# Delta rule's output projection: norm gain moved into the weights, the gate product on GpSimd, the squares on VectorE, two weight units split in quarters

## The chip, the cores and the metric

The kernel runs on one core of a Trainium2 chip. The metric is the device time of one execution in microseconds (us), here the median of three runs. A core has TensorE (matrix products; PE in the profile, PEld for its weight loads), ScalarE (ACT), VectorE (DVE), GpSimd (POOL) and SyncE (SP), which here only issues DMAs. Each engine works through its own queue in order, and the queues meet only at semaphores.

## The reference, cut to what matters

The whole program is two transformer blocks over 16 + 512 = 528 tokens of width 1024. The change lies in the last part of the first layer, the output of the gated delta rule:

```
def gated_deltanet(h, w_in, w_conv, a_log, dt_bias, w_norm, w_out):
    ...
    o = chunk_gated_delta_rule(q, k, v, g, beta)          # (1, 528, 16 heads, 128)
    o = rms_norm(o, w_norm) * jax.nn.silu(z.reshape(b, t, GDN_V_HEADS, GDN_HEAD_DIM).astype(jnp.float32))
    return o.reshape(b, t, GDN_V_DIM).astype(h.dtype) @ w_out

def rms_norm(x, w):
    y = xf * lax.rsqrt(jnp.mean(xf * xf, axis=-1, keepdims=True) + RMS_EPS)
    return (y * w.astype(jnp.float32)).astype(x.dtype)
```

`w_norm` is one vector of 128 gains, the same for all 16 heads; `w_out` is 2048 x 1024. The result is added to the residual `h`. Everything is float32.

## The kernel before, in words

Features lie on the 128 partitions and the 528 tokens on the free axis, so one head's output is a tile of 128 x 528, `value(i)` for head i of 16, in `k.wide`. A float32 product is made of three products of rounded halves: weights and activations are each split into a high part (rounded by ScalarE) and a low part (the rest, by VectorE), and TensorE multiplies high by high, high by low and low by high (`product`, L174). Weights come in units of 128 x 2048 in a ring of four raw slots (`load_unit`, L130). `split_hi` (L151) and `split_lo` (L159) make the high and the low part of a unit, in two split slots.

`gdn_back` runs the delta rule itself. Near its end it replaces the spilled gate z in DRAM by z(1 + tanh(z/2)), which is twice silu(z), and it loads the first three units of `w_out` ahead.

`normed_down` (L2217) is the stage around the change. For each head i: a square of `value(i)` on ScalarE (`square`), its sum over the 128 features by two matmuls with a matrix of ones on TensorE (`total`, L2342), a logarithm and an exponential on ScalarE (`logarithm`, L2265, and `root`, L2269) which give 1/rms, value times gain times 1/rms on VectorE (`norm`, L2301), that times 0.5 times the loaded gate (`scale`, L2308) into `a`, then the high part of `a` on ScalarE (L2280) and the low part on VectorE (`low`, L2312). TensorE multiplies head i into output tile 0 (weight unit 0) as soon as its low part is there, and head i - 3 into output tile 1 (unit 1; `BEHIND` is 3), then issues `total(i+3)`:

```
            for kt in range(kts):
                pe.wait_ge(lo_ready, kt + 1)
                one(0, kt)
                if kt == BEHIND:
                    pe.wait_ge(k.lo_done, u0 + 2)
                if kt >= BEHIND:
                    one(1, kt - BEHIND)
                if kt + 3 < kts:
                    total(kt + 3)
```

Units 2 to 7 follow with all 16 heads each; their splits wait until the unit two before has been used. The order of each queue is written out by hand. The gates come by 16 DMAs into a ring of four slots, each behind the `scale` that frees its slot. The gain vector is loaded at the start of the stage.

Of the kernel before, what the change touches and what calls it, by code (L numbers as in the profile page):

```python
# [23 lines left out]
P = 128  # L24
# [27 lines left out]
def persistent(nc, ctx):  # L52

    k = Named(nc=nc)
    sb = lambda name, shape, dt=F32: ctx.enter_context(nc.sbuf_tensor(name, shape, dt))
    sem = lambda name: ctx.enter_context(nc.semaphore(name))
    k.stage_sems, k.last_sems, k.uncleared = ExitStack(), ExitStack(), []
    k.opened = []

    def stage_sem(name):  # L60

        k.opened.append(k.stage_sems.enter_context(nc.semaphore(name)))
        return k.opened[-1]
# [6 lines left out]
    k.eps = sb("eps", [P, 1])  # L70
    k.gains_in = sem("gains_in")
# [1647 lines left out]
def gdn_back(k, g, qkv, an, d, tmp, yt, chunk, out_unit):  # L1719
# [13 lines left out]
    with ExitStack() as ctx:  # L1733
# [15 lines left out]
                 "y5_done", "xz6_ready", "xz6_done", "y6_ready", "y6_done", "cut", "stepped", "one", "zeroed", "back", "tanh_done", "gated", "gate_stored")  # L1749
# [18 lines left out]
        def _(sp):  # L1768
# [415 lines left out]
def gdn(k, ins):  # L2184
# [3 lines left out]
    with ExitStack() as c:  # L2188
# [13 lines left out]
        gdn_back(k, g, qk, an, d, tmp, yt, chunk, gdn_out_unit(ins))  # L2202


def gdn_out(k, ins, then):
# [3 lines left out]
    normed_down(k, "gdn_out", gdn_out_unit(ins), ins["gdn_norm"].rearrange("o p -> p o"), k.z_d, o, k.h,  # L2209
# [7 lines left out]
def normed_down(k, name, cols, gain_src, gate_d, value, acc, later_gains, then=()):  # L2217
# [4 lines left out]
    with ExitStack() as ctx:  # L2222
        sb = lambda nm, shape, dt=F32: ctx.enter_context(nc.sbuf_tensor(f"{name}_{nm}", shape, dt))
        ahi, alo = sb("ahi", [P, kts, T], F32R), sb("alo", [P, kts, T], F32R)
        sq, rinv, z, a, gain = sb("sq", [P, 3, T]), sb("rinv", [P, 3, T]), sb("z", [P, ZS, T]), sb("a", [P, 2, T]), sb("gain", [P, 1])
# [3 lines left out]
        gain_in, squared, summed, log, inv, normed, scaled, hi_ready, lo_ready, added = (k.sem(f"{name}_{x}") for x in (  # L2229
            "gain_in", "squared", "summed", "log", "inv", "normed", "scaled", "a_hi", "a_lo", "added"))  # L2230
# [3 lines left out]
        ring = lambda u: (u0 + u) % RAW_SLOTS  # L2234

        @block.sync
        def _(sp):
            with nc.allow_non_contiguous_dma(reason="128 gains, feature on partitions"):
                sp.dma_start(gain[:, :], gain_src).then_inc(gain_in, 16)
# [14 lines left out]

        @block.scalar
        def _(act):
            def square(i):
                if i >= 3:
                    act.wait_ge(summed, i - 2)
                nc.scalar.activation(sq[:, i % 3, :], value(i), ACT.Square).then_inc(squared, 1)  # L2260
            def logarithm(i):
# [5 lines left out]
            def root(i):  # L2267
# [4 lines left out]
            square(1)  # L2272
            logarithm(0)
            root(0)
            square(2)
            logarithm(1)
# [12 lines left out]
            for u in range(n):  # L2289
                if u + 2 <= n:  # L2290
                    split_hi(k, act, u0 + u + 2, ring(u + 2), t0 + u + 1)
                if u >= 1:
                    tail.act(k, act, u - 1, added, u)
            tail.act(k, act, n - 1, added, n)
# [3 lines left out]
        def _(dve):  # L2298
            def norm(i):
                dve.wait_ge(inv, i + 1)  # L2300
                dve.scalar_tensor_tensor(out=rinv[:, i % 3, :], in0=value(i), scalar=gain[:, 0:1], in1=rinv[:, i % 3, :],  # L2301
                                         op0=ALU.mult, op1=ALU.mult).then_inc(normed, 1)
            def scale(i):
                dve.wait_ge(normed, i + 1)
                dve.wait_ge(z_in[i % ZS], 16 * (i // ZS) + 16)
                if i >= 2:
                    dve.wait_ge(lo_ready, i - 1)
                dve.scalar_tensor_tensor(out=a[:, i % 2, :], in0=rinv[:, i % 3, :], scalar=0.5, in1=z[:, i % ZS, :],  # L2308
                                         op0=ALU.mult, op1=ALU.mult).then_inc(scaled, 1)
# [3 lines left out]
            split_lo(k, dve, u0, ring(0))  # L2313
            dve.wait_ge(gain_in, 16)
            norm(0)
            for i in range(kts):
                if i >= 2:
                    low(i - 1)
                if i == BEHIND + 1:
                    split_lo(k, dve, u0 + 1, ring(1))  # L2320
                scale(i)
                if i == 0:
                    low(0)
                if i + 1 < kts:
                    norm(i + 1)
            low(kts - 1)
            for u in range(n):
                dve.wait_ge(k.tile_full, t0 + u + 1)
                dve.tensor_tensor(two(acc[:, u, :]), two(acc[:, u, :]), halves(k.ps[u % 4]), ALU.add).then_inc(added, 1)
                if u + 2 <= n:  # L2330
                    split_lo(k, dve, u0 + u + 2, ring(u + 2))
# [4 lines left out]
        def _(pe):  # L2336
# [16 lines left out]
            pe.wait_ge(k.lo_done, u0 + 1)  # L2353
# [1665 lines left out]
```

## Time and profile before

| | us |
|---|---|
| median of three runs | 1987.78 |
| the three runs | 1982.62, 1987.78, 1988.21 |
| span of the profiled execution, first to last instruction | 1984.7 |
| stage `normed_down`: first instruction to the end of its first two output tiles, in the span | 504.4 to 564.2 |

No device time of its own is listed for the profiled execution; its span stands 3.1 us under the median of the runs. Times in the trace count from the start of the span. A time in brackets behind a row is how long the engine sat idle before it, and the name behind the arrow is what it was waiting for. The column PEclk is the granted clock of TensorE as a share of 2.4 GHz. An instruction is often reported until some 0.08 us after its successor on the same engine has begun.

### The profile page before, as it was taken

How to read it: one execution, taken by the hardware profiler on the slowest of the kernel's cores; microseconds unless marked ns; L12 is line 12 of the kernel's file. 1: busy time of each engine (PE TensorE's matmuls, PEld its weight loads, DVE VectorE, ACT ScalarE, POOL GpSimd, SP SyncE). 2: the span in 40 equal slices, each digit the busy share in tenths (PEclk: the TensorE clock that was granted, in tenths of full speed). 3: DMA queues.
4: the chain of work that ended last, by engine and by line, in shares of the span. 5: the costliest groups of instructions: out<-in, count | busy, mean ns of one | idle time of the engine just before them, and what ended most of it. 6: DMA issues, size and time to landing. Idle time of an engine off the chain costs nothing. (4 is left out here: it accounts for less than half of the span.)

```text
span 1984.7 us, 31477 instructions
## 1 busy us (share of the span) xinstructions
PE 1891.1 (95%) x12756; PEld 1695.5 (85%) x12756; DVE 1076.6 (54%) x1786; ACT 871.5 (44%) x1437; POOL 111.1 (6%) x140
## 2 busy tenths in 40 slices
PE   7999999999799999999989998999999998899988
PEld 6999999898689999999989976778888885787766
DVE  6656689976543444444452277444444446853343
ACT  5557763677633433332243256343232333424442
POOL 0001150000000000000000020000000002000101
PEclk8999999999899999999999998999999998999989
DMA  7233462255342232222222232132323222411101
GB/s 175 86 92 105 130 190 71 63 160 167 100 118 84 86 98 94 85 85 97 93 62 90 71 83 84 64 106 85 106 85 104 86 85 66 125 46 43 49 17 43
DMA packets 211359, 182.58 MB, mean 92 GB/s; under 512 B 42736, under 2 KB 182000, under 8 KB 211240
## 3 DMA queue, kind: packets, MB, share of 16 engines
q1 hardware_dynamic: 211240, 180.93, 30.5%
q8 instruction: 83, 1.36, 0.3%
q14 instruction: 36, 0.29, 0.0%
HBM read 165.73 MB, written 15.16 MB: 91 GB/s over the span
## 5 line engine op out<-in xcount | busy, mean ns | idle before, releaser
L163 DVE TENSOR_TENSOR main_wlo<-raw,main_whi 128x2048 fp32r<-128x2048 f32 x106 | 244.1, 2302 | 348.0 <-ACT main_whi L156 348.0
L156 ACT CAST main_whi<-raw 128x2048 fp32r<-128x2048 f32 x106 | 201.7, 1903 | 408.4 <-PE ps L178 408.4
L178 PE MATMUL ps<-ffn_xhi,main_whi 128*128 128x264 f32 (+1 forms) x768 | 206.0, 322 | 6.6 <-DVE ffn_xlo L648 6.6
L178 PE MATMUL ps<-ffn_xhi,main_wlo 128*128 128x264 f32 (+1 forms) x768 | 206.1, 323 | 0.0
L178 PE MATMUL ps<-ffn_xlo,main_whi 128*128 128x264 f32 (+1 forms) x768 | 205.8, 322 | 0.0
L178 PE MATMUL ps<-ffn_ahi,main_wlo 128*128 128x264 f32 (+1 forms) x768 | 205.2, 322 | 0.0
L178 PE MATMUL ps<-ffn_alo,main_whi 128*128 128x264 f32 (+1 forms) x768 | 205.0, 321 | 0.0
L178 PE MATMUL ps<-ffn_ahi,main_whi 128*128 128x264 f32 (+1 forms) x768 | 203.9, 320 | 0.0
L178 PE MATMUL ps<-gdn_xhi,gdnf_whi 128*128 128x264 f32 x768 | 161.8, 292 | 4.4 <-DVE gdn_xlo L519 4.4
L178 PE MATMUL ps<-gdn_xlo,gdnf_whi 128*128 128x264 f32 x768 | 157.1, 286 | 0.0
L178 PE MATMUL ps<-gdn_xhi,gdnf_wlo 128*128 128x264 f32 x768 | 157.1, 286 | 0.0
L178 PEld LDWEIGHTS ps<-ffn_xhi,main_whi 128*128 128x128 f32 x768 | 129.0, 190 | 19.1 <-issue 7.5
L178 PEld LDWEIGHTS ps<-ffn_ahi,main_whi 128*128 128x128 f32 x768 | 127.9, 188 | 11.6
L178 PEld LDWEIGHTS ps<-ffn_xhi,main_wlo 128*128 128x128 f32 x768 | 128.4, 190 | 11.0
L178 PEld LDWEIGHTS ps<-ffn_xlo,main_whi 128*128 128x128 f32 x768 | 127.9, 189 | 11.5 <-issue 0.2
L178 PEld LDWEIGHTS ps<-ffn_ahi,main_wlo 128*128 128x128 f32 x768 | 127.7, 188 | 10.9
L178 PEld LDWEIGHTS ps<-ffn_alo,main_whi 128*128 128x128 f32 x768 | 126.9, 188 | 11.2
L361 DVE TENSOR_TENSOR h<-h,ps 128x528 f32<-128x528 f32 (+1 forms) x128 | 85.6, 692 | 80.2 <-PE ps L178 80.0
L178 PEld LDWEIGHTS ps<-gdn_xhi,gdnf_whi 128*128 128x128 f32 x768 | 121.6, 190 | 5.8 <-issue 4.8
L178 PEld LDWEIGHTS ps<-gdn_xlo,gdnf_whi 128*128 128x128 f32 x768 | 120.2, 190 | 0.0
L178 PEld LDWEIGHTS ps<-gdn_xhi,gdnf_wlo 128*128 128x128 f32 x768 | 119.8, 190 | 0.0
L1089 DVE SCALAR_TENSOR_TENSOR gdnf_y<-gdnf_pre,gdnf_convw,gdnf_y 128x528 f32<-128x528 f32 x96 | 82.6, 862 | 62.4 <-ACT gdnf_y L1062 60.0
(498 smaller groups left out, 3717.9 us busy)
## 6 DMA issues: line engine op xcount, KB each, us to landing
raw<-in_ff_up_dram SPq DMA_DIRECT2D x32, 1024.0 KB, 5.4
raw<-in_ff_down_dram SPq DMA_DIRECT2D x32, 1024.0 KB, 5.0
raw<-in_gdn_in_dram SPq DMA_DIRECT2D x24, 1024.0 KB, 5.5
raw<-in_w_in_dram SPq DMA_DIRECT2D x14, 1024.0 KB, 5.3
raw<-in_mlstm_in_dram SPq DMA_DIRECT2D x12, 1024.0 KB, 5.4
raw<-in_gdn_out_dram SPq DMA_DIRECT2D x8, 1024.0 KB, 7.2
gdn_v_spilled<-gdn_o SPq DMA_DIRECT2D x16, 264.0 KB, 2.2
gdn_z_spilled<-gdn_o SPq DMA_DIRECT2D x16, 264.0 KB, 3.5
```

The costliest lines, as they stand in the source:

```text
L156: k.nc.scalar.copy(k.whi[:, slot % SPLIT_SLOTS, :], k.raw[:, slot, :]).then_inc(k.hi_done, 1)
L163: eng.tensor_tensor(k.wlo[:, s, :], k.raw[:, slot, :], k.whi[:, s, :].bitcast(F32), ALU.subtract).then_inc(k.lo_done, 1)
L178: mm = pe.matmul(ps[:, b, 0:k.width], w, x[:, half], start=first and n == 0, stop=last and n == 2)
L361: dve.tensor_tensor(parted(k, acc[:, j, k.now]), parted(k, acc[:, j, k.now]), filled(k, k.ps[j % 4]), ALU.add).then_inc(s.down_free, 1)
L1089: dve.scalar_tensor_tensor(out=self.y[:, b, :], in0=self.pre[:, b, i:i + T], scalar=self.w[:, i, j:j + 1], in1=self.y[:, b, :], op0=ALU.mu ...
```

## The change

The gain vector no longer multiplies the activations. It lies along the rows of `w_out` within each head, so it is folded into the weights when they are split: the high part is the rounding of gain times weight (ScalarE, an activation with a scale vector), the low part is gain times weight minus that (VectorE). The factor 0.5 is put into the gain once by GpSimd, and the gain is loaded in `gdn_back`, behind its first loads on the SP queue. The product of value and gate moves to GpSimd, in place over the gate; VectorE makes the squares that ScalarE made, and one product of 1/rms with that result in place of two instructions. Units 0 and 1 are split in four quarters of 512 columns each (four heads' weights), one quarter at the start and one behind every second head, in the order unit 0, unit 1, unit 0, ...; TensorE waits for the quarter that it needs. `scale(i+1)` now stands ahead of `low(i)` on VectorE. Whole units 2 to 7 are split as before, with the gain.

```
 # gdn_back
+            with nc.allow_non_contiguous_dma(reason="128 gains, feature on partitions"):
+                sp.dma_start(k.out_gain[:, :], out_gain).then_inc(s.gain_in, 16)
...
+            pool.wait_ge(s.gain_in, 16)
+            pool.tensor_scalar(k.out_gain[:, :], k.out_gain[:, :], 0.5, None, ALU.mult).then_inc(s.gain_half, 1)
 # normed_down
+        quarter = lambda x: (x % 2, slice(UNIT // 4 * (x // 2), UNIT // 4 * (x // 2 + 1)))
...
+        @block.gpsimd
+        def _(pool):
+            for i in range(kts):
+                pool.wait_ge(z_in[i % ZS], 16 * (i // ZS) + 16)
+                pool.tensor_tensor(z[:, i % ZS, :], z[:, i % ZS, :], value(i), ALU.mult).then_inc(gated, 1)
 # ScalarE
-            square(0)
-            split_hi(k, act, u0, ring(0), t0)
...
+            weight_part(0)
             root(0)
             root(1)
             for i in range(kts):
                 act.wait_ge(scaled, i + 1)
                 nc.scalar.copy(hi(i), a[:, i % 2, :]).then_inc(hi_ready, 1)
                 if i + 2 < kts:
-                    logarithm(i + 2)
-                if i + 3 < kts:
-                    square(i + 3)
-                if i + 2 < kts:
                     root(i + 2)
-                if i == BEHIND - 1:
-                    split_hi(k, act, u0 + 1, ring(1), t0)
+                if i % 2 == 0 and i < 14:
+                    weight_part(i // 2 + 1)
 # VectorE
+            def square(i):
+                if i >= 3:
+                    dve.wait_ge(summed, i - 2)
+                dve.tensor_tensor(sq[:, i % 3, :], value(i), value(i), ALU.mult).then_inc(squared, 1)
...
+            def scale(i):
+                dve.wait_ge(gated, i + 1)
                 dve.wait_ge(inv, i + 1)
...
+                dve.tensor_tensor(a[:, i % 2, :], z[:, i % ZS, :], rinv[:, i % 3, :], ALU.mult).then_inc(scaled, 1)
...
+            square(0)
+            square(1)
+            weight_part(0)
+            square(2)
+            scale(0)
             for i in range(kts):
+                if i % 2 == 1 and i < 14:
+                    weight_part((i + 1) // 2)
                 if i + 1 < kts:
-                    norm(i + 1)
+                    scale(i + 1)
+                low(i)
+                if i + 3 < kts:
+                    square(i + 3)
+            weights(2)
 # TensorE
             for kt in range(kts):
+                if kt % 4 == 0:
+                    split(kt // 2)
                 pe.wait_ge(lo_ready, kt + 1)
                 one(0, kt)
-                if kt == BEHIND:
-                    pe.wait_ge(k.lo_done, u0 + 2)
                 if kt >= BEHIND:
+                    if (kt - BEHIND) % 4 == 0:
+                        split((kt - BEHIND) // 2 + 1)
                     one(1, kt - BEHIND)
```

## Rows read from the trace of the kernel before

**Rows 1.** Page, part 1: busy time of each engine, share of the span.
```profile
PE 1891.1 (95%) x12756; PEld 1695.5 (85%) x12756; DVE 1076.6 (54%) x1786; ACT 871.5 (44%) x1437; POOL 111.1 (6%) x140
```

**Rows 2.** Windows: busy PE, PEld, DVE, ACT, POOL; then PEclk, DMA share, GB/s.
```profile
506.00:516.00 10.00, 7.80 (x22) 5.63 (x22) 7.78 (x9) 7.47 (x13) 0.00 (x0) 0.51 0.89 266
516.00:523.00 7.00, 3.89 (x19) 2.72 (x18) 3.38 (x5) 6.80 (x11) 0.00 (x0) 0.97 0.29 77
523.00:530.00 7.00, 6.26 (x23) 5.54 (x24) 4.93 (x6) 2.81 (x6) 0.00 (x0) 0.52 0.27 80
530.00:561.00 31.00, 26.93 (x168) 22.17 (x168) 20.76 (x31) 21.92 (x39) 0.00 (x0) 1.00 0.45 121
```

**Rows 3.** Groups by line in the stage: busy us, mean ns; idle before, releaser.
```profile
L2301 DVE SCALAR_TENSOR_TENSOR gdn_out_rinv<-wide,gdn_out_gain,gdn_out_rinv 128x528 f32<-128x528 f32 x16 | 12.3, 767 | 13.3 <-ACT gdn_out_rinv L2269 13.3
L2308 DVE SCALAR_TENSOR_TENSOR gdn_out_a<-gdn_out_rinv,gdn_out_z 128x528 f32<-128x528 f32 x16 | 11.2, 702 | 0.1
L2265 ACT ACTIVATE gdn_out_rinv<-ps,eps 128x528 f32<-128x528 f32 x16 | 11.2, 700 | 10.4 <-PE ps L2342 10.4
L2260 ACT ACTIVATE gdn_out_sq<-wide 128x528 f32<-128x528 f32 x16 | 10.2, 636 | 0.9 <-PEq L97 0.9
L2269 ACT ACTIVATE gdn_out_rinv<-gdn_out_rinv 128x528 f32<-128x528 f32 x16 | 10.2, 635 | 0.1
```

**Rows 4.** Timeline of one head in the steady part of the stage.
```profile
545.45 1.05 PE L2342 MATMUL ps<-gdn_out_sq,ones 128*128 128x264 f32 x4
546.11 0.70 DVE L2312 TENSOR_TENSOR gdn_out_alo<-gdn_out_a,gdn_out_ahi 128x528 fp32r<-128x528 f32 x1
546.54 0.70 ACT L2265 ACTIVATE gdn_out_rinv<-ps,eps 128x528 f32<-128x528 f32 x1 [0.63 <-PE ps L2342]
...
546.87 0.51 PE L178 MATMUL ps<-gdn_out_ahi,main_whi 128*128 128x264 f32 x2 [0.36 <-DVE gdn_out_alo L2312]
...
548.45 1.05 PE L2342 MATMUL ps<-gdn_out_sq,ones 128*128 128x264 f32 x4
```

**Rows 5.** Timeline: `low` of heads 0, 5, 13 and 15.
```profile
511.48 0.71 DVE L2312 TENSOR_TENSOR gdn_out_alo<-gdn_out_a,gdn_out_ahi 128x528 fp32r<-128x528 f32 x1 [0.95 <-ACT gdn_out_ahi L2280]
...
531.33 0.70 DVE L2312 TENSOR_TENSOR gdn_out_alo<-gdn_out_a,gdn_out_ahi 128x528 fp32r<-128x528 f32 x1
...
554.94 0.70 DVE L2312 TENSOR_TENSOR gdn_out_alo<-gdn_out_a,gdn_out_ahi 128x528 fp32r<-128x528 f32 x1
...
559.54 0.71 DVE L2312 TENSOR_TENSOR gdn_out_alo<-gdn_out_a,gdn_out_ahi 128x528 fp32r<-128x528 f32 x1 [0.70 <-ACT gdn_out_ahi L2280]
```

**Rows 6.** Timeline: unit 2's low half, and the first product behind it.
```profile
563.34 2.29 DVE L163 TENSOR_TENSOR main_wlo<-raw,main_whi 128x2048 fp32r<-128x2048 f32 x1 [1.29 <-ACT main_whi L156]
...
565.69 0.51 PE L178 MATMUL ps<-gdn_out_ahi,main_whi 128*128 128x264 f32 x2 [1.46 <-DVE main_wlo L163]
```

**Rows 7.** SP's first DMA issues in the stage; the gate tile's times to landing.
```profile
504.49 0.33 SPq L2239 DMA_DIRECT2D gdn_out_gain<-in_gdn_norm_dram  x1
504.87 1.37 SPq L2246 DMA_DIRECT2D gdn_out_z<-gdn_z_spilled  x3
...
DMA to landing us min/median/max: 2.4/2.7/7.5
```

**Rows 8.** Timeline: GpSimd and VectorE, each with two inputs in SBUF.
```profile
278.63 1.29 POOL L1405 TENSOR_TENSOR gdnf_y<-gdnf_y,gdn_an 128x512 f32<-128x512 f32 x1 [1.26 <-DMA gdnf_y<-gdn_cum_rows]
280.25 2.97 POOL L1405 TENSOR_TENSOR gdnf_y<-gdnf_y,gdn_an 128x512 f32<-128x512 f32 x1 [0.33 <-DMA gdnf_y<-gdn_cum_rows]
...
278.72 3.35 DVE L163 TENSOR_TENSOR gdnf_wlo<-raw,gdnf_whi 128x2048 fp32r<-128x2048 f32 x1 [0.47 <-ACT gdnf_whi L156]
```

**Rows 9.** Groups by form elsewhere: instructions like the new ones.
```profile
L3854 POOL TENSOR_TENSOR fin_sqs<-fin_sqs,fin_sq 128x512 f32<-128x512 f32 x5 | 6.4, 1289 | 26.3 <-ACT fin_sq L3830 26.3
...
L633 ACT ACTIVATE ffn_xhi<-h,gains 128x528 fp32r<-128x528 f32 x8 | 5.1, 722 | 7.7 <-PEq L97 7.7
...
L648 DVE SCALAR_TENSOR_TENSOR ffn_xlo<-h,gains,ffn_xhi 128x512 fp32r<-128x512 f32 x8 | 5.4, 748 | 1.1 <-ACT ffn_xhi L633 1.1
```

More of the change, by code:

```diff
@@ L70, in persistent @@
     k.eps = sb("eps", [P, 1])
+    k.out_gain = sb("gdn_out_gain", [P, 1])
     k.gains_in = sem("gains_in")
@@ L2214, with normed_down @@
 ZS = 4
-def normed_down(k, name, cols, gain_src, gate_d, value, acc, later_gains, then=()):
+def normed_down(k, name, cols, gate_d, value, acc, later_gains, then=()):
     nc = k.nc
@@ L2234, in normed_down @@
         ring = lambda u: (u0 + u) % RAW_SLOTS
+        gain = k.out_gain[:, 0:1]
+        quarter = lambda x: (x % 2, slice(UNIT // 4 * (x // 2), UNIT // 4 * (x // 2 + 1)))
+        whole = lambda x: x - 6 + u0 + 1
         @block.sync
         def _(sp):
-            with nc.allow_non_contiguous_dma(reason="128 gains, feature on partitions"):
-                sp.dma_start(gain[:, :], gain_src).then_inc(gain_in, 16)
             for i in range(kts):
@@ L2253, in _, with weight_part, weights, root @@
             sp.wait_ge(k.gains_in, 16 * len(later_gains))
+        @block.gpsimd
[3 more added lines that the diff above has]
+                pool.tensor_tensor(z[:, i % ZS, :], z[:, i % ZS, :], value(i), ALU.mult).then_inc(gated, 1)
         @block.scalar
         def _(act):
[L2257 to L2261, printed above, removed]
+            def weight_part(x):
+                u, cs = quarter(x)
+                if x < 2:
+                    act.wait_ge(k.raw_landed[ring(u)], landed_value(u0 + u, ring(u)))
+                    act.wait_ge(k.tile_full, t0)
+                nc.scalar.activation(k.whi[:, ring(u) % SPLIT_SLOTS, cs], k.raw[:, ring(u), cs], ACT.Copy, scale=gain)\
+                    .then_inc(part_hi if x < 6 else k.hi_done, 1)
+            def weights(u, used):
+                act.wait_ge(k.raw_landed[ring(u)], landed_value(u0 + u, ring(u)))
+                act.wait_ge(k.tile_full, used)
+                nc.scalar.activation(k.whi[:, ring(u) % SPLIT_SLOTS, :], k.raw[:, ring(u), :], ACT.Copy, scale=gain)\
+                    .then_inc(k.hi_done, 1)
+            def root(i):
                 act.wait_ge(summed, i + 1)
@@ L2281, in _ @@
                 if i + 2 < kts:
-                    logarithm(i + 2)
-                if i + 3 < kts:
-                    square(i + 3)
-                if i + 2 < kts:
                     root(i + 2)
-                if i == BEHIND - 1:
-                    split_hi(k, act, u0 + 1, ring(1), t0)
[L2289 to L2294, printed above, removed]
+                if i % 2 == 0 and i < 14:
+                    weight_part(i // 2 + 1)
+            for u in range(2, n):
+                weights(u, t0 + u - 1)
+                if u >= 3:
+                    tail.act(k, act, u - 3, added, u - 2)
+            split_hi(k, act, u0 + n, ring(n), t0 + n - 1)
+            for u in range(n - 3, n):
+                tail.act(k, act, u, added, u + 1)
             tail.root(k, act)
@@ L2298, in _, with weight_part, weights @@
         def _(dve):
-            def norm(i):
-                dve.wait_ge(inv, i + 1)
[L2301 to L2305, printed above, removed]
+            def square(i):
+                if i >= 3:
+                    dve.wait_ge(summed, i - 2)
+                dve.tensor_tensor(sq[:, i % 3, :], value(i), value(i), ALU.mult).then_inc(squared, 1)
+            def weight_part(x):
+                u, cs = quarter(x)
+                if x < 6:
+                    dve.wait_ge(part_hi, x + 1)
+                else:
+                    dve.wait_ge(k.hi_done, whole(x))
+                w = ring(u) % SPLIT_SLOTS
+                dve.scalar_tensor_tensor(out=k.wlo[:, w, cs], in0=k.raw[:, ring(u), cs], scalar=gain,
+                                         in1=k.whi[:, w, cs].bitcast(F32), op0=ALU.mult, op1=ALU.subtract)\
+                    .then_inc(part_lo if x < 6 else k.lo_done, 1)
+            def weights(u):
+                s = ring(u) % SPLIT_SLOTS
+                dve.wait_ge(k.hi_done, u0 + u + 1)
+                dve.scalar_tensor_tensor(out=k.wlo[:, s, :], in0=k.raw[:, ring(u), :], scalar=gain,
+                                         in1=k.whi[:, s, :].bitcast(F32), op0=ALU.mult, op1=ALU.subtract).then_inc(k.lo_done, 1)
+            def scale(i):
+                dve.wait_ge(gated, i + 1)
+                dve.wait_ge(inv, i + 1)
                 if i >= 2:
                     dve.wait_ge(lo_ready, i - 1)
-                dve.scalar_tensor_tensor(out=a[:, i % 2, :], in0=rinv[:, i % 3, :], scalar=0.5, in1=z[:, i % ZS, :],
-                                         op0=ALU.mult, op1=ALU.mult).then_inc(scaled, 1)
+                dve.tensor_tensor(a[:, i % 2, :], z[:, i % ZS, :], rinv[:, i % 3, :], ALU.mult).then_inc(scaled, 1)
             def low(i):
@@ L2352, in _, with split @@
                 total(i)
-            pe.wait_ge(k.lo_done, u0 + 1)
+            def split(x):
+                if x < 6:
+                    pe.wait_ge(part_lo, x + 1)
+                else:
+                    pe.wait_ge(k.lo_done, whole(x))
             for kt in range(kts):
+                if kt % 4 == 0:
+                    split(kt // 2)
                 pe.wait_ge(lo_ready, kt + 1)
                 one(0, kt)
-                if kt == BEHIND:
-                    pe.wait_ge(k.lo_done, u0 + 2)
                 if kt >= BEHIND:
+                    if (kt - BEHIND) % 4 == 0:
+                        split((kt - BEHIND) // 2 + 1)
                     one(1, kt - BEHIND)
```

37 lines of the change are left out of this document (12 added, 25 removed).

## The prediction

> **What bounds the kernel now.** I read the page first: TensorE is busy 95% of the span [rows 1], so time can be saved only where it waits. The windows around the edited stage show such a place. From 530 to 561 us TensorE is busy 26.93 of 31 us at full clock; from 506 to 516 and from 523 to 530 it runs at about half its clock (0.51 and 0.52), the second time after a stretch (516 to 523) in which it had only 3.89 us of work in 7 [rows 2]. The groups of the stage then give each instruction's price [rows 3], and the timeline of one head gives the loop. There neither engine is full: ScalarE waits 0.63 us for TensorE's total, TensorE waits 0.36 us for `low` [rows 4]. The bound is a chain through all queues: total, logarithm, exponential, the VectorE steps, product, total. `low` of head 5 starts at 531.33 and that of head 15 at 559.54 [rows 5]: 28.2 / 10 = 2.82 us a head, 5.64 for two. TensorE's own work for a head is 1.05 (total) and two products; from 546.87 to the next total at 548.45 these take 1.58 after a wait [rows 4]; I take 1.46 without one, as the first matmuls behind a wait report 0.51 and the others 0.41. So 2.51 is its floor, and at most 0.3 us a head is to be had once the clock is up.
>
> The sum is made against the span of 1984.7; the median of the runs is 3.1 us above it, and I carry the difference over to the median. A measurement of this kernel can tell about 0.3% from no change, that is 5.96 us.
>
> **The change part by part.**
>
> *Work by engine.* ScalarE loses 16 squares of 0.636 and the whole splits of units 0 and 1, and gains eight quarters. A scaled rounding of 528 columns takes 0.722 [rows 9]; I take 0.71 for 512. VectorE loses `norm` (0.767) and gains a square, taken at `scale`'s 0.70 [rows 3]: even. Its quarters cost 0.75, the row of the same instruction at 512 columns [rows 9], against 2.29 for a whole unit [rows 6]: 8 x 0.75 = 6.0 against 4.6, so 1.4 us more over the stage. GpSimd gets 16 products. It takes 1.29 for 512 columns [rows 9], so about 1.3.
>
> *The new loop, without GpSimd.* What matters is the order. `low(i)` stands behind `scale(i+1)`, which needs the root of head i+1; at every odd i a quarter stands in front of both, and that quarter's high part stands on ScalarE behind that same root. Queued behind them are the next square on VectorE and the next `hi` on ScalarE, and TensorE waits for `low(i)`. From the end of `total(i+1)`: handoff 0.04, logarithm 0.70, handoff 0.04, exponential 0.635, quarter's high part 0.71 less 0.09 overlap, handoff 0.04, quarter's low part 0.75 less 0.08, `scale` 0.70 less 0.08, `low` 0.70: sum 4.07. (The handoff is the gap between a releaser's end and the start behind it: the total ends at 546.50, the logarithm starts at 546.54 [rows 4].) From the end of `low` to the end of the total that closes the loop: 0.05 + 1.58 + 1.05 = 2.68. Together 6.75 us, and it closes every two heads, since that total is `total(i+3)`. Before it was 5.64. So each pair of heads loses 1.1 us although no engine has more work than time: VectorE has 6 x 0.62 + 0.67 = 4.4 of 6.75.
>
> *Stretch by stretch, without GpSimd.* (a) To head 0's `low`: the gain's DMA no longer stands ahead of the gates (0.38 us [rows 7]), so gate 0 is issued at 504.49 and lands at about 507.2 with the median 2.7; its product with the value takes 1.3, then `scale(0)`, and `low(0)` must wait for `scale(1)`, whose gate lands a little later. That gives `low(0)` at 511 to 512.5 against 511.48: 0. (b) Heads 0 to 5 took 19.85 us before [rows 5], with a whole split between them and the second cold spell. The new loop makes it two loops of 6.75 and one head of 3.4, 16.9; but the first cold spell stays, and at half clock TensorE's 2.51 becomes about 5 for each head that has both products. I take -1.5, with 0 and -3 as ends. (c) Heads 5 to 13: four pairs, 4 x 1.1 = +4.4. (d) Behind head 13 there are no quarters, squares or gates left. Before, `low` of 13 ended at 555.64 and the two tiles at 564.2, 8.56 us; the nine products left are 9 x 0.735 = 6.6, with waits about 7. I take -1.5. (e) Units 2 to 7: the split of unit 2 is exposed now (TensorE waits 1.46 [rows 6]) and gets the scaled forms, 0.09 on ScalarE (0.722 with a scale vector [rows 9] against 0.635 for an activation of such a tile without one [rows 3]) and at most 0.06 on VectorE: +0.15. The others lie behind 16 x 0.735 = 11.8 us of products each. Sum: 0 - 1.5 + 4.4 - 1.5 + 0.15 = +1.6.
>
> *GpSimd and VectorE together.* At 278.72 VectorE began a 2048-column subtraction 0.09 us after GpSimd had begun a product of 1.29. It took 3.35; the same form takes 2.29 [rows 6, 8]. GpSimd's next product began at 280.25, ended at 283.22 and so ran 2.97, of which 1.15 lay after VectorE's end at 282.07 [rows 8]. So here one waits until the other is through, and each meeting costs 1.06 to 1.15 us. Every VectorE instruction of the new loop has two inputs in SBUF. VectorE's 4.4 and two GpSimd products (2.2) fill 6.6 of 6.75, so the products cannot all miss the chain. Ends: nothing (all in gaps) and 16 x 1.1 = 17.6 (all on the chain). The chain uses VectorE for 2.0 of each 6.75, and the products start when a gate lands, at no fixed phase; I take 2.0 / 6.75 of 17.6, some 5, less what the last heads absorb and what the cold start covers: +3.5.
> The Trainium skill (SBUF — State Buffer, Reading the diagram) says that the port pair which GpSimd and VectorE share is an exclusive lock, which a VectorE instruction with two SBUF inputs takes against a GpSimd instruction that reads SBUF. By this rule all 16 products exclude VectorE, as in my sum; without it the sum would be +1.6. The trace agrees, with 3.35 for 2.29.
>
> *Costed at nothing.* The gain's load and its halving in `gdn_back`: one DMA on SP behind loads that are followed by a wait for spilled gates, and one tiny GpSimd instruction on an idle engine; if that cover were gone it would cost one landing, 2.4 to 7.5 [rows 7]. Gates: a slot is free four heads (13 us) ahead, and landing plus product take 2.7 + 1.3. Loads of units 4 to 7 follow the same gates on SP and have more than 30 us.
>
> Forecast: 1.6 + 3.5 = +5.1, so 1984.7 + 5.1 = 1989.8 of span, 1992.9 as a median.
>
> **The rivals.**
>
> *A, the forecast:* the two-head loop with the quarters in it, and the meetings. With its ends (stretch b -3 to 0, meetings 1.5 to 7) +1.6 to +9: 1989 to 1997.
>
> *B, the meetings cost nothing,* since the products fall into VectorE's gaps of 2.35 us a loop. +1.6: 1989.4. For: the gaps are there. Against: 6.6 of 6.75.
>
> *C, TensorE becomes the bound (faster).* The small quarters keep it fed, its clock rises at 516 and never falls, and the queues run ahead. From 512.2: three heads of 1.8 and thirteen of 2.51, three products: 512.2 + 5.4 + 32.6 + 2.2 = 552.4, plus 2 for the cold start, against 564.2: -10, 1978. For: the old stretch at 0.35 a head over the floor and the cold spell at 523. It decides if `low` of odd heads comes within 2.5 us of the total before last; by rows 3, 4 and 9 it takes 4.07. If the quarters alone slip off the chain, loops are 5.4 to 5.7, and the result is near -3.
>
> *D, the clock falls again.* TensorE's share in the new loop is 5.0 / 6.75 = 0.74 against 0.87 before, with one gap of about 1.7 us in each pair. The spell at 523 followed 3.89 / 7 = 0.56 [rows 2]. A spell of 7 us at half clock takes in 7 / 5.0 = 1.4 heads, each 5.0 - 3.4 = 1.6 us longer than the loop: 2.2 a spell, and two or three more spells add 4 to 7. +9 to +12: 1997 to 2000. Against: at 0.87 in this stage, and through a head with 0.36 us of idle time in it, the clock held [rows 2, 4].
>
> *E, no effect:* 1987.8, if the gains at both ends cancel the loop. It lies between B and C.
>
> **How the numbers follow.** A 0.52, B 0.11, C 0.12, D 0.14, E 0.11. The time is A's, 1992.9. 80% range: it leaves out C's far half and D's upper end: 1983 to 1999. A's own range is 1989 to 1997. Bounds of no change are 1981.8 and 1993.7. Faster: C less its weak form, 0.10. Slower: D, and somewhat under half of A, 0.38. Same: the rest, 0.52.
>
> **What the profile after would show.** `low` of even and odd heads in pairs, unevenly spaced, with about 7 us per pair between 530 and 555; VectorE idle until ScalarE's quarter; a quarter-sized VectorE instruction or a `scale` of 1.5 us or more where a GpSimd product overlaps; GpSimd products of 1.3, some 2; TensorE at about 0.72 in the stage; unit 2's products starting at about 570 instead of 565.7; everything behind that shifted alone. I would be wrong if `low` came every 2.5 us (C), if the total ran at half clock behind 530 (D), or if another stage moved.

## The result and the profile after

| | us |
|---|---|
| changed kernel, median of 14 runs | 1993.49 (1991.04 to 1997.76) |
| kernel before, median of 14 runs on the same chip | 1985.81 (1981.9 to 1993.4) |
| ratio | 1.0041, 95% interval 1.003 to 1.0051 |
| span of the changed kernel's profiled execution | 1994.0 |

The changed kernel is slower by 0.41%, 7.7 us between the medians. The forecast was 1992.9. It had a chance of 0.52 on "within 0.3%", and the result lies just beyond that bound. In every profiled run of the experiments the device time stands 1.7 us above the span, so the profiled execution of before took about 1986.4. A profile is one execution and can lie several us from the median: 2.2 above it for after, 7.1 below it for the second profile of before, 5.8 below it for "VectorE's quarter behind `low`".

The busy times of the page, beside [rows 1]: TensorE's is the same, VectorE's is 9.6 us more, ScalarE's 5.7 less and GpSimd's 23.5 more:

```profile
PE 1891.5 (95%) x12756; PEld 1697.6 (85%) x12756; DVE 1086.2 (54%) x1792; ACT 865.8 (43%) x1427; POOL 134.6 (7%) x157
```

The windows that answer to [rows 2] (same columns). The stage begins 3.8 us later in this profile: ScalarE's first instruction of it starts at 508.19, where it started at 504.36.

```profile
506.00:516.00 10.00, 3.77 (x18) 2.53 (x16) 7.41 (x11) 5.70 (x10) 4.29 (x3) 0.94 0.69 203
516.00:523.00 7.00, 5.12 (x17) 3.90 (x17) 7.00 (x7) 3.05 (x6) 5.52 (x4) 0.50 0.41 130
523.00:530.00 7.00, 4.00 (x14) 2.56 (x14) 5.72 (x6) 4.04 (x7) 2.75 (x2) 0.85 0.14 40
530.00:561.00 31.00, 23.51 (x131) 20.69 (x132) 19.29 (x30) 17.54 (x29) 11.60 (x8) 0.89 0.27 74
```

Between 530 and 561 us TensorE was busy 26.93 of 31 at full clock before. Now it is busy 23.51, at a granted clock of 0.89. From 516 to 523 VectorE is busy the whole 7.00 us with only seven instructions.

The groups of the stage that answer to [rows 3] (busy us, mean ns, then idle time before and its releaser):

```profile
L2266 POOL TENSOR_TENSOR gdn_out_z<-gdn_out_z,wide 128x528 f32<-128x528 f32 x16 | 24.2, 1523 | 180.5 <-DMA gdn_out_z<-gdn_z_spilled 180.5
...
L179 PE MATMUL ps<-gdn_out_ahi,main_whi 128*128 128x264 f32 x76 | 18.9, 332 | 19.6 <-DVE gdn_out_alo L2338 18.0 <-DVE main_wlo L2328 1.6
...
L2335 DVE TENSOR_TENSOR gdn_out_a<-gdn_out_z,gdn_out_rinv 128x528 f32<-128x528 f32 x16 | 16.6, 1044 | 1.7 <-POOL gdn_out_z L2266 1.6
...
L2338 DVE TENSOR_TENSOR gdn_out_alo<-gdn_out_a,gdn_out_ahi 128x528 fp32r<-128x528 f32 x16 | 12.3, 768 | 0.1
L2314 DVE TENSOR_TENSOR gdn_out_sq<-wide 128x528 f32<-128x528 f32 x16 | 12.2, 769 | 0.3 <-PEq L98 0.3
L2286 ACT ACTIVATE gdn_out_rinv<-ps,eps 128x528 f32<-128x528 f32 x16 | 11.1, 697 | 22.7 <-PE ps L2370 22.7
...
L2322 DVE SCALAR_TENSOR_TENSOR main_wlo<-raw,gdn_out_gain,main_whi 128x512 fp32r<-128x512 f32 x8 | 6.7, 835 | 15.2 <-ACT main_whi L2275 15.2
```

TensorE waits 18.0 us for `low` (L2338). `scale` (L2335) takes 1044 ns in the mean, where such an instruction took 702. VectorE waits 15.2 us for ScalarE's quarters, which is mostly the order's doing. Below, a collision is a VectorE instruction that stands still while GpSimd works. The next view is the timeline of one series of them. GpSimd makes four products in 6.61 us, and the VectorE instructions beside them take 1.80 instead of 0.70:

```profile
517.48 6.61 POOL L2266 TENSOR_TENSOR gdn_out_z<-gdn_out_z,wide 128x528 f32<-128x528 f32 x4 [2.21 <-DMA gdn_out_z<-gdn_z_spilled]
...
517.66 1.80 DVE L2335 TENSOR_TENSOR gdn_out_a<-gdn_out_z,gdn_out_rinv 128x528 f32<-128x528 f32 x1
...
519.39 1.80 DVE L2338 TENSOR_TENSOR gdn_out_alo<-gdn_out_a,gdn_out_ahi 128x528 fp32r<-128x528 f32 x1
...
521.12 1.81 DVE L2314 TENSOR_TENSOR gdn_out_sq<-wide 128x528 f32<-128x528 f32 x1
...
522.85 1.80 DVE L2335 TENSOR_TENSOR gdn_out_a<-gdn_out_z,gdn_out_rinv 128x528 f32<-128x528 f32 x1
```

Later there are cold stretches (TensorE at half clock) that the kernel before did not have in this place. Here a total takes 1.97 us, where one at full clock takes 1.05 [rows 4]. GpSimd's products beside it hold nobody up: the first begins inside VectorE's square and takes 1.60 instead of 1.30, and both are through before VectorE's wait of 3.37 us ends:

```profile
537.44 0.51 PE L179 MATMUL ps<-gdn_out_ahi,main_whi 128*128 128x264 f32 x2 [2.14 <-DVE gdn_out_alo L2338]
...
539.16 0.69 DVE L2314 TENSOR_TENSOR gdn_out_sq<-wide 128x528 f32<-128x528 f32 x1
539.19 1.97 PE L2370 MATMUL ps<-gdn_out_sq,ones 128*128 128x264 f32 x4
539.41 1.60 POOL L2266 TENSOR_TENSOR gdn_out_z<-gdn_out_z,wide 128x528 f32<-128x528 f32 x1 [3.82 <-DMA gdn_out_z<-gdn_z_spilled]
...
541.19 0.70 ACT L2286 ACTIVATE gdn_out_rinv<-ps,eps 128x528 f32<-128x528 f32 x1 [3.76 <-PE ps L2370]
...
541.50 1.31 POOL L2266 TENSOR_TENSOR gdn_out_z<-gdn_out_z,wide 128x528 f32<-128x528 f32 x1 [0.49 <-DMA gdn_out_z<-gdn_z_spilled]
...
543.22 0.75 DVE L2322 SCALAR_TENSOR_TENSOR main_wlo<-raw,gdn_out_gain,main_whi 128x512 fp32r<-128x512 f32 x1 [3.37 <-ACT main_whi L2275]
```

The only VectorE instruction that is held up between heads 5 and 13 in this profile is one quarter, at 549.94:

```profile
549.94 1.04 DVE L2322 SCALAR_TENSOR_TENSOR main_wlo<-raw,gdn_out_gain,main_whi 128x512 fp32r<-128x512 f32 x1 [2.26 <-ACT main_whi L2275]
```

Behind the stage the products begin at unit 2, which answers to [rows 6]:

```profile
573.37 2.35 DVE L2328 SCALAR_TENSOR_TENSOR main_wlo<-raw,gdn_out_gain,main_whi 128x2048 fp32r<-128x2048 f32 x1 [3.89 <-ACT main_whi L2280]
...
575.78 0.52 PE L179 MATMUL ps<-gdn_out_ahi,main_whi 128*128 128x264 f32 x2 [1.63 <-DVE main_wlo L2328]
```

From ScalarE's first instruction of the stage to the end of unit 2's low half ("the stage" below) it is 67.5 us, against 61.3 before (504.36 to 565.63). So the stage gives +6.3 of the 9.3 us by which the two spans differ. It is cut by the starts of `low` of heads 0, 5 and 13, as in [rows 5]:

| | to head 0 | 0 to 5 | 5 to 13 | behind 13 | stage |
|---|---|---|---|---|---|
| before | 7.1 | 19.85 | 23.6 | 10.7 | 61.3 |
| before, profiled a second time | 7.0 | 18.1 | 23.6 | 10.6 | 59.3 |
| after | 7.6 | 20.9 | 29.8 | 9.2 | 67.5 |
| after, profiled a second time | 7.7 | 21.1 | 29.8 | 9.2 | 67.8 |
| product on 16 of 528 columns (an experiment below) | 5.3 | 16.1 | 26.9 | 10.7 | 59.0 |

### The profile page after: what moved, and what is told of

It reads as the page before. It is cut to its first block and busy times, and to the rows that moved or that the text cites. A ratio compares the mean times of both kernels' runs of the same rounds, so it can differ in the third digit from the quotient of the medians.

```text
span 1994.0 us, 31492 instructions
## 1 busy us (share of the span) xinstructions
PE 1891.5 (95%) x12756; PEld 1697.6 (85%) x12756; DVE 1086.2 (54%) x1792; ACT 865.8 (43%) x1427; POOL 134.6 (7%) x157
## 5 line engine op out<-in xcount | busy, mean ns | idle before, releaser
L164 DVE TENSOR_TENSOR main_wlo<-raw,main_whi 128x2048 fp32r<-128x2048 f32 x98 | 225.7, 2303 | 336.6 <-ACT main_whi L157 336.6
L157 ACT CAST main_whi<-raw 128x2048 fp32r<-128x2048 f32 x98 | 186.5, 1903 | 368.4 <-PE ps L179 368.4
```

Source lines behind the costliest of these rows:

```text
L157: k.nc.scalar.copy(k.whi[:, slot % SPLIT_SLOTS, :], k.raw[:, slot, :]).then_inc(k.hi_done, 1)
L164: eng.tensor_tensor(k.wlo[:, s, :], k.raw[:, slot, :], k.whi[:, s, :].bitcast(F32), ALU.subtract).then_inc(k.lo_done, 1)
```

## The experiments

Every ratio is to the kernel before on the same chip. They were measured in three groups of four, in the order below, in which the median of before was 1986.77, 1984.64 and 1985.01. A stage's length is read from one profiled execution. "Loop" is the time from one `low` of an odd head to the next, in the steady part.

**No product at all.**

```
-        @block.gpsimd
-            ... pool.tensor_tensor(z[:, i % ZS, :], z[:, i % ZS, :], value(i), ALU.mult).then_inc(gated, 1)
             def scale(i):
-                dve.wait_ge(gated, i + 1)
+                dve.wait_ge(z_in[i % ZS], 16 * (i // ZS) + 16)
```

The value is left out of the result here, which is gate times 1/rms alone.

> The changed kernel without GpSimd's product: the normalised value is left out of the result, which is gate times 1/rms alone; all else stays. Theory 1 (order and exclusion: the quarters make a two-head loop of 6.7 us, and GpSimd's products hold VectorE up on top of it): the 9 products that met VectorE go, the loops stay at 6.7, the stage ends some 6 to 10 us sooner than in the changed kernel, so 1984 to 1988 where the kernel before is at 1986. Rival 2 (the products cost nothing, only the order does): no more than 1 us less than the changed kernel's 1993.5. Rival 3 (cold TensorE spells are the loss, and come from something else): low spacing unchanged, a gain only as large as the cold spells that happen to be missing.

Measured: 1989.39, ratio 1.0012 (1.0001 to 1.0023), stage 60.2. The stage is 7.3 us shorter, as the first theory had it; the time lies 1.4 us above its range. The loop of two heads on VectorE:

```profile
535.76 0.75 DVE L2316 SCALAR_TENSOR_TENSOR main_wlo<-raw,gdn_out_gain,main_whi 128x512 fp32r<-128x512 f32 x1 [2.25 <-ACT main_whi L2269]
...
537.05 0.70 DVE L2332 TENSOR_TENSOR gdn_out_alo<-gdn_out_a,gdn_out_ahi 128x528 fp32r<-128x528 f32 x1
...
538.90 0.70 DVE L2332 TENSOR_TENSOR gdn_out_alo<-gdn_out_a,gdn_out_ahi 128x528 fp32r<-128x528 f32 x1
...
542.50 0.75 DVE L2316 SCALAR_TENSOR_TENSOR main_wlo<-raw,gdn_out_gain,main_whi 128x512 fp32r<-128x512 f32 x1 [2.27 <-ACT main_whi L2269]
...
543.78 0.70 DVE L2332 TENSOR_TENSOR gdn_out_alo<-gdn_out_a,gdn_out_ahi 128x528 fp32r<-128x528 f32 x1
```

From 537.05 to 543.78 is 6.73, where the prediction had summed 6.75, and VectorE waits 2.27 in it for the quarter's high half. No instruction is stretched.

**The product on VectorE.** GpSimd's block is taken out.

```
+            def gate(i):
+                dve.wait_ge(z_in[i % ZS], 16 * (i // ZS) + 16)
+                dve.tensor_tensor(z[:, i % ZS, :], z[:, i % ZS, :], value(i), ALU.mult).then_inc(gated, 1)
             square(2)
+            gate(0)
             scale(0)
+            gate(1)
...
                     square(i + 3)
+                if i + 2 < kts:
+                    gate(i + 2)
```

> The changed kernel with the product of value and gate on VectorE, behind the next square, in place of GpSimd. VectorE gets 16 x 0.62 = 9.9 us more work. Theory 1: it has 6.7 - 4.4 = 2.3 us idle in each two-head loop and the two products (1.24) fit into it behind the chain, while each exclusion of 1.1 to 1.3 us goes: 6 to 9 us less than the changed kernel, 1984 to 1988. Rival 2: VectorE is only loaded further; no gain or up to 5 us more than the changed kernel.

Measured: 1990.46, ratio 1.0018 (1.0008 to 1.0028), stage 59.4. The time is 2.5 us above the expected range. VectorE has 16 more instructions of 0.70 us, and the stage is as short as with no product. They fill the wait for the quarter, which falls from 2.25 to 0.91, and the loop stays 6.73:

```profile
543.70 0.70 DVE L2335 TENSOR_TENSOR gdn_out_alo<-gdn_out_a,gdn_out_ahi 128x528 fp32r<-128x528 f32 x1
...
549.14 0.75 DVE L2316 SCALAR_TENSOR_TENSOR main_wlo<-raw,gdn_out_gain,main_whi 128x512 fp32r<-128x512 f32 x1 [0.91 <-ACT main_whi L2269]
...
550.43 0.70 DVE L2335 TENSOR_TENSOR gdn_out_alo<-gdn_out_a,gdn_out_ahi 128x528 fp32r<-128x528 f32 x1
```

**VectorE's quarter behind `low`.**

```
-                if i % 2 == 1 and i < 14:
-                    weight_part((i + 1) // 2)
                 if i + 1 < kts:
                     scale(i + 1)
                 low(i)
+                if i % 2 == 1 and i < 14:
+                    weight_part((i + 1) // 2)
```

> The changed kernel with VectorE's quarter behind low(i) instead of ahead of scale(i+1). No work is added or removed. Theory 1: the quarter's two steps (0.62 on ScalarE, 0.71 on VectorE with its handoff) leave the chain total, root, scale, low; the quarter's high part still delays hi, so a loop of about 6.0 in place of 6.7: 0.7 x 6 loops = 4 us less, 1989 to 1991. Rival 2 (VectorE's and GpSimd's work together is the bound, 6.6 of 6.7, and order is nothing): under 1 us of difference.

Measured: 1993.63, ratio 1.0035 (1.0022 to 1.0049), stage 62.9, loops 6.9. The expectation failed: the loop was to be 6.0, and the time 1989 to 1991. Between heads 5 and 13 seven VectorE instructions are held up by 1.1 us each, where after has one of 0.3, and so collisions took part of what the order gave. The profiled execution (1987.83) was the fastest of its eight, and its stage says little of the median.

**Both quarters moved,** ScalarE's also ahead of `root(i + 2)`.

```
+                if i % 2 == 0 and i < 14:
+                    weight_part(i // 2 + 1)
                 if i + 2 < kts:
                     root(i + 2)
-                if i % 2 == 0 and i < 14:
-                    weight_part(i // 2 + 1)
```

> As e3, and ScalarE's quarter also ahead of the root, into the time in which ScalarE waits for the total (22.7 us over 9 waits in the changed kernel). Theory 1: a loop of about 5.4 to 5.7 but for the meetings with GpSimd; 6 us less than the changed kernel, 1986 to 1989, where the exclusion (6.6 us of VectorE and GpSimd for two heads) now sets the pace. Rival 2 (pure work of both engines): as e3, under 1 us.

Measured: 1991.32, ratio 1.0024 (1.0011 to 1.0036), stage 62.4, loops 6.6. The time is 2.3 us above the expected range. The quarters are off the chain and yet the loop is hardly shorter than the 6.73 without a product. The windows, then one loop on VectorE, say why:

```profile
530.00:550.00 20.00, 15.93 (x103) 13.73 (x102) 19.98 (x23) 13.26 (x22) 8.43 (x6) 1.00 0.30 83
```
```profile
543.88 1.79 DVE L2335 TENSOR_TENSOR gdn_out_a<-gdn_out_z,gdn_out_rinv 128x528 f32<-128x528 f32 x1
545.60 0.70 DVE L2338 TENSOR_TENSOR gdn_out_alo<-gdn_out_a,gdn_out_ahi 128x528 fp32r<-128x528 f32 x1
...
548.74 1.83 DVE L2314 TENSOR_TENSOR gdn_out_sq<-wide 128x528 f32<-128x528 f32 x1
550.54 1.76 DVE L2335 TENSOR_TENSOR gdn_out_a<-gdn_out_z,gdn_out_rinv 128x528 f32<-128x528 f32 x1
```

VectorE is busy or held up 19.98 of 20 us. Its own 4.4 us and two collisions of 1.1 make the 6.6 of the loop: it has become the bound.

**The product on VectorE and both quarters moved.**

> The changed kernel with the product of value and gate on VectorE and both quarters moved (e2 and e4 together). Without exclusion and with the quarter off the chain, Theory 1 gives a loop of 0.04 + 0.70 + 0.04 + 0.64 + 0.04 + 0.62 + 0.70 + 2.68 = 5.5 us for two heads against 6.7 in e2: 6 loops x 1.2 = 7 us less in the stage than e2 (59.4 us to the end of unit 2's low half), so 52 to 53, and 1983 to 1984 as a time; faster than the kernel before if what stands outside of the stage is the same. Rival 2 (VectorE's load sets the pace: 6 x 0.62 + 2 x 0.62 + 0.67 = 5.6 a loop): the same pace from another cause, told apart by whether VectorE idles.

Measured: 1985.47, ratio 0.9995 (0.9984 to 1.0006), stage 55.4, loops 5.86. The window of the same stretch:

```profile
530.00:550.00 20.00, 17.40 (x108) 14.19 (x106) 19.76 (x32) 15.45 (x26) 0.00 (x0) 1.00 0.34 96
```

VectorE does 32 instructions in the time in which it did 23. So each edit alone leaves a bound of 6.6 to 6.7, and the two together take both away. The time is 1.5 us above what was expected, and the stage 2.4. VectorE is busy 19.76 of 20 us, so its own load (5.6 us a loop by the sum in the expectation) now sets the pace, as the rival had it. The stage is 4 to 6 us shorter than before's 61.3 and 59.3, but the median is not. Nor does that gain come from the loop: between heads 5 and 13 this version takes 23.45 us and before took 23.6. It comes from heads 0 to 5, 14.65 against 19.85 and 18.1.

**Before, with only the early gain.** The tensor `gdn_out_gain` among the lasting ones, its load and its halving in `gdn_back`; nothing uses it.

> The kernel before with nothing but the gain's early load in gdn_back and its halving on GpSimd added (the result isn't used; the stage is untouched). In the profiles of the changed kernel, e1, e2 and e4 the stage began 3 to 4 us later than before, behind two cold spells of TensorE at 349 and 414 us. If the early load brings these about: 3 to 4 us slower than before. If they are chance, and lie in the kernel before's runs as often: no difference within 1 us.

Measured: 1989.78, ratio 1.0019 (1.0008 to 1.003), stage 60.4. Both cold stretches are there, 3.4 us each, at 352 and 417. The first is no sign of the early load: the unchanged kernel's second profile has it too, at 350. The second it has not.

**The product over 16 of 528 columns.** The value is left out of the other 512.

> The changed kernel with GpSimd's product over the first 16 of 528 columns only: the rest of the value is left out of the result. All waits stay. Theory 1 (GpSimd keeps VectorE out while it works): as e1, about 4 to 5 us less than the changed kernel, loops of 6.7. Rival 2 (the handoff gate, GpSimd, VectorE costs by itself): like the changed kernel.

Measured: 1986.57, ratio 1.001 (0.9996 to 1.0024), stage 59.0. GpSimd's instructions and waits are all there, but they take 346 ns instead of 1523, and `scale` is back at 704:

```profile
L2335 DVE TENSOR_TENSOR gdn_out_a<-gdn_out_z,gdn_out_rinv 128x528 f32<-128x528 f32 x16 | 11.3, 704 | 3.0 <-POOL gdn_out_z L2266 1.5 <-ACT gdn_out_rinv L2289 1.4
...
L2266 POOL TENSOR_TENSOR gdn_out_z<-gdn_out_z,wide 128x16 f32<-128x16 f32 x16 | 5.5, 346 | 187.8 <-DMA gdn_out_z<-gdn_z_spilled 187.8
```

So what costs is the length of GpSimd's products, and not the handover through a third engine. In the time it is 1.001 against 1.0041 (1.0047 in the last run), some 6 us, which is clear of the 0.17% noted below. Between heads 5 and 13 the clock is full throughout; a cold stretch of 3.4 us lies behind head 13, at 554.6.

**Before again,** unchanged.

> The kernel before once more, for a second profile. If the cold spells at 349 and 414 us are chance, they may stand in this profile too, and the stage begins near 508 instead of 504; the stage itself is 61 us long to the end of unit 2's low half, give or take a cold spell of 2 us.

Measured: 1988.21, ratio 1.0017 (1.0005 to 1.0028). An identical kernel read 0.17% slower, so the intervals are too narrow and differences under about 0.2% say nothing. The verdicts above on the early gain (1.0019) and on the absent product (1.0012) are therefore not measured in the time; I read them from the traces. In those traces, all kernels that hold the 4-byte gain tensor show something in a stage that the change does not touch. First after, then before profiled again (VectorE's transposes, and TensorE's wait for two of them):

```profile
L1533 DVE STREAM_TRANSPOSE raw<-gdn_d 32x1024 f32<-32x1024 f32 x8 | 18.2, 2277 | 0.3
...
414.97 0.51 PE L1905 MATMUL ps<-ident,raw 96*96 96x96 f32 x4 [1.59 <-DVE raw L1533]
```
```profile
L1532 DVE STREAM_TRANSPOSE raw<-gdn_d 32x1024 f32<-32x1024 f32 x8 | 16.3, 2032 | 0.3
...
413.30 0.51 PE L1900 MATMUL ps<-ident,raw 96*96 96x96 f32 x4 [1.10 <-DVE raw L1532]
```

Three of the last four runs asked whether the tensor's place or its early load does that.

**After, gain tensor of 64 bytes a partition.**

```
-    k.out_gain = sb("gdn_out_gain", [P, 1])
+    k.out_gain = sb("gdn_out_gain", [P, 16])[:, 0:1]
```

> The changed kernel whole, but the halved gain's tensor holds 64 bytes of a partition instead of 4 (its first column is used), so that all tensors placed behind it lie where a multiple of 64 bytes puts them. If the place of the tensors is what lengthened the stream transposes of 32x1024 (2032 ns before, about 2275 ns in every kernel that has the 4-byte tensor), they take 2030 ns again, TensorE's wait for them near 413 us is 1.10 us instead of 1.59, no cold spell of 3.4 us follows there, and the median is 2 to 4 us under that of the changed kernel, about 1990.5. If the early transfer or the early halving is the cause, the transposes stay at 2275 ns and the time at 1993. The stage of the heads is untouched by it: 66 to 68 us.

Measured: 1993.11, ratio 1.0036 (1.0024 to 1.0047), stage 65.7. The load and the halving are as early as before, and the transposes are short again:

```profile
L1533 DVE STREAM_TRANSPOSE raw<-gdn_d 32x1024 f32<-32x1024 f32 x8 | 16.3, 2034 | 0.3
...
413.59 0.51 PE L1905 MATMUL ps<-ident,raw 96*96 96x96 f32 x4 [1.09 <-DVE raw L1533]
```

So the place of the tensors behind it is the cause of the slow transposes. In the time this version is 1.7 us below the last run (1993.11 and 1994.85), which is under the noise, and its stage alone was 2 us shorter; the 2 to 4 us that I had expected are not there.

**The best version with 64 bytes.** The product on VectorE and both quarters moved, with the wider tensor.

> The version with the product on VectorE and both first quarters moved behind the low halves, with the 64-byte gain tensor. Its stage took 55.4 us against 59.3 to 61.3 of the kernel before, yet its time was no shorter (0.9995). If the place of the tensors took that gain away upstream, the transposes are back at 2030 ns and the median is 2 to 4 us under the kernel before, ratio 0.998 to 0.9985. If not, transposes 2280 ns and ratio 0.9995 again.

Measured: 1983.94, ratio 0.9994 (0.9983 to 1.0005), stage 54.4. The transposes are 2034 ns, but the ratio did not move: that expectation failed.

**The best version with 60 bytes.**

> As the version before it, but the gain's tensor holds 60 bytes, so that it and the 4-byte constant ahead of it make 64. If only the shift against the kernel before counts (a multiple of 64 wanted), the transposes are slow, about 2275 ns, with a wait of 1.59 us near 413; if what counts is that later tensors start on a multiple of 64 bytes, they are as fast as 2030 ns or faster. If the place does not matter at all, this kernel and the one with 64 bytes give the same duration as the one with 4.

Measured: 1982.73, ratio 0.9985 (0.9973 to 0.9997), stage 54.4, transposes 2030 ns. It is the fastest version, yet its 0.15% is less than what the kernel before differed from itself. 60 bytes do as well as 64, so it isn't the shift by itself that counts; which addresses are bad stays open.

**After again,** on the chip of the last three.

> The changed kernel again, unchanged, on the same chip as the three above, to set the padded one beside it. An unchanged kernel before read 1.0017 of itself, so a difference under about 0.2% says nothing. Expected: ratio 1.003 to 1.005, transposes 2275 ns.

Measured: 1994.85, ratio 1.0047 (1.0031 to 1.0063), stage 67.8, transposes 2275 ns.

## Why the prediction was right in its time, and where its steps were off

The time came within 0.6 us (1993.49 for 1992.9), and both halves of the forecast's mechanism are in the trace. But much of that is luck. The forecast difference was +5.1 and the measured one +7.7. The base that it was added to, 1987.78 from three runs, lay 2.0 above the median of fourteen. And the terms were off in opposite directions. (The ends given for rival A add up to +10, not +9; nothing rests on it.)

*The new loop, without GpSimd: right, 6.73 for 6.75.* The quarter in front of `scale` and `low` costs what the sum said: VectorE waits 2.25 us for it in each pair.

*Stretch (c), +4.4: too large, +3.3.* The 5.64 a pair of the kernel before was a mean up to head 15, which takes in the quick last heads. In the stretch itself it was 23.6 / 4 = 5.9 a pair. With the product over 16 columns the stretch takes 26.9.

*Stretches (a) and (b), 0 and -1.5: too small a gain.* With the 16-column product they take 5.3 and 16.1, that is -1.8 and -3.7 against the first profile of before and -1.7 and -2.0 against the second. *Stretch (d), -1.5: right at full clock.* It takes 9.2 in all three profiles of after (the padded one with them), against 10.7 before. With the 16-column product and with none it takes 10.7, but both profiles have 3.4 us of cold clock there. (e)'s +0.15 is right (TensorE waits 1.63 for 1.46). All told, the order alone gives a stage of 59.0 to 60.2, late cold stretch included, against 61.3 and 59.3. I had +1.6; it is between -2.3 and +0.9, about nothing.

*GpSimd and VectorE together, +3.5: the term that was mis-sized.* A collision costs what was said: 1.80 - 0.70 = 1.10. The Trainium skill (SBUF — State Buffer, Reading the diagram) says that whichever of the two starts first has the shared ports for its whole instruction, and that the other fully blocks; the trace agrees, with 1.80 for 0.70 on VectorE and, the other way round, 1.60 for 1.30 on GpSimd. But the stage with full products takes 67.5 and 67.8 and with small ones 59.0, so they cost 8.6 (6.7 in the padded version). In VectorE's groups of after the stretching is 16 x (1.044 - 0.704) = 5.4 in `scale`, 1.0 each in `low` and the square and 0.7 in the quarters, 8.1 in all. That is seven collisions of 1.10 in which VectorE was the one held up (five of them hit `scale`, which is on the chain) and two of 0.3 to 0.4 in quarters.

I had weighted all 17.6 us by the chain's share of the loop, 0.30, as if the products started at no fixed phase, and had taken some off for the cold start. Both steps fail. All seven collisions lie ahead of 530 us, in stretches (a) and (b), where VectorE has few gaps (7.00 busy of 7 from 516 to 523), and there they cost nearly their full length: 7.6 + 20.9 against 5.3 + 16.1 is 7.1. TensorE's clock matters little there: the second profile of after had 6.9 us more of half clock in this place and took 0.3 longer. In the loop itself the sum "6.6 of 6.75, so the products cannot all miss the chain" came out the other way: between heads 5 and 13 VectorE is held up by 0.29 us in one profile of after and 0.40 in the other (0.8 in the padded version). The products fall into its wait for the quarter. That the gate's issue, which follows `scale`, fixes this phase is argued from the code and was not tested by itself. With both quarters moved the phase was another one, and the same two instructions were held up in every loop, 6.6 us apart.

*Rival D, the clock, came on top of A.* The stage of after has cold stretches of 3.4 us at 538.7 and 552.4 behind one of 10.2 from 514.8. In the other profile it is 13.7 from 513.4, and 3.4 at 537.3 and 550.9. Stretch (c) is 29.8 in both, against 26.9 with small products and at full clock. The two pairs of heads with a cold stretch take 7.82 and 8.28, the two without 7.01 and 6.73, where 6.73 is the loop of the experiment. So of the 2.9 some 2.6 is clock and 0.3 is collision. The padded version has one cold stretch there instead of two, and takes 28.6. The two may be linked. With small products or none, TensorE's wait for `low` is 1.74 to 1.76 us in each pair between heads 5 and 13, and the clock held there (behind head 13 it fell once in both, after the same wait). In the three profiles of after the wait is 2.05 to 2.30 in seven pairs, six of them behind a quarter that a product had held up by 0.3 to 0.6, and in five of the seven the clock fell within 1.6 us of the wait's end. So the small collisions may bring the cold stretches about; nothing tested that by itself. One sign I had named as proof against me, a total at half clock behind 530, did occur. The forecast had A and D as alternatives, where they belong together.

*"Costed at nothing": wrong in its reason.* The early load and halving show no cost of their own (in the padded version, which has them, the stage begins at 504.19, where before's began at 504.36), but the 4-byte tensor moved others, and eight transposes take 0.24 us longer each, 1.9 in all on VectorE and 0.5 on TensorE's wait. "Another stage moved" was the other sign against me, and it occurred too. What this is worth in the 7.7 us is not shown: the padded version came out 1.7 lower, which is under the noise. The stage is 67.65 against 60.3 in the means of two profiles each, which is 7.4.

*E falls,* by the measured 0.41%. *B falls as a whole,* since full products cost 8.6 us in the stage, but in the loop it was right: there the products fell into VectorE's gaps. *C falls:* TensorE was never the bound of the loop, not even at 5.86 (busy 17.40 of 20).

*Open: where the best version's gain goes.* Three kernels with a stage 4 to 7 us shorter gave 0.15% at best. Part of it is seen. In some executions each weight tile far behind the stage takes 11.75 us instead of 11.68 (below), and the two profiles that had the slower pace lost 30 x 0.07 = 2 us to it. A cold stretch that begins between 1014 and 1025 us lasts 10.2 to 13.7 us in these versions, and 6.8 in both profiles of before. Whether that follows from the earlier end of the stage or is chance was not tested; it is 10.2 as well in the version without a product, whose stage is 4.8 to 5.8 us longer than theirs.

## What to carry to other kernels

Work moved from VectorE to an idle GpSimd isn't free when both read two operands in SBUF: here seven of 16 products held VectorE up for 1.10 us each, to save it instructions of 0.70. What decides is where VectorE has gaps. At the start of the stage it had few, and the collisions cost nearly their full length; in the steady loop it had a wait of 2.25 us, and they held it up by 0.3 us in four pairs of heads. Look for a place in VectorE's own waits first. Before writing a piece of work into the loop, list what stands behind it on each queue: a quarter that no one needs for four heads stood ahead of the step that everyone waits for. Taking away one bound of 6.7 us showed another of 6.6 behind it, and only both edits together brought the loop to 5.9, which is no more than the kernel before had. And run the unchanged kernel again as if it were an experiment, before small differences are believed.

## What the runs showed of the hardware that was not expected

*A stream transpose of 32 x 1024 depends on where its tensors lie.* VectorE's eight transposes of `gdn_d` into `raw` took 2.03 us each in before, and with 60 or 64 bytes added ahead; 2.27 to 2.28 us with 4 bytes added, in each of the nine profiles that had them. The other four of this shape, from `gdn_an` to `gdn_d`, stayed at 1.93 to 1.98 us in all fourteen. In seven of the nine, TensorE's clock also fell for 3.4 us between 414 and 418, where its wait had grown from 1.10 to 1.59; in the five profiles without the shift it never did. The windows, first of after again, then of the padded version:

```profile
410.00:421.00 11.00, 9.41 (x79) 8.85 (x79) 8.52 (x18) 4.76 (x14) 0.00 (x0) 0.84 0.72 193
```
```profile
410.00:421.00 11.00, 9.91 (x98) 9.36 (x98) 8.69 (x18) 6.65 (x18) 0.00 (x0) 1.00 0.69 191
```

*The same kernel runs its matmuls at two slightly different paces.* In the long stage from 650 to 1000, TensorE is never idle and at full clock, and one weight tile follows the other every 11.75 us in one profile of after and every 11.68 in the other, unchanged over 30 tiles. Before changed from the slower to the faster pace between two stages of one execution. ScalarE's timeline, first of after, then of after again:

```profile
768.91 1.91 ACT L157 CAST main_whi<-raw 128x2048 fp32r<-128x2048 f32 x1 [9.84 <-PE ps L179]
780.66 1.91 ACT L157 CAST main_whi<-raw 128x2048 fp32r<-128x2048 f32 x1 [9.84 <-PE ps L179]
```
```profile
769.09 1.91 ACT L157 CAST main_whi<-raw 128x2048 fp32r<-128x2048 f32 x1 [9.77 <-PE ps L179]
780.77 1.91 ACT L157 CAST main_whi<-raw 128x2048 fp32r<-128x2048 f32 x1 [9.77 <-PE ps L179]
```

The slower pace stands in eight of the fourteen profiles, the faster in six. Over the stage it makes 2 us, one of the reasons why runs of one kernel differ.
